# Gate weights split earlier, and the second half of the first four units taken unit by unit

## The reference

```
x = x + 0.5 * rmsnorm(swiglu(rmsnorm(x, g[4]), w_in, w_out), g[5])      # feed-forward
gate = sigmoid(rmsnorm(x, g[6]) @ ple_w_gate)                           # 1024 x 1024
x = x + rmsnorm(gate * (p @ ple_w_proj), g[7])                          # 256 x 1024
```

```
h = h + 0.5 * swiglu(rms_norm(h, norm_ffn2), w_ffn2_in, w_ffn2_out)
gate = sigmoid(rms_norm(h, norm_ple) @ w_ple_gate)
h = h + gate * (p @ w_ple_proj)
```

## Time and profile before

| | |
|---|---|
| median of 3 executions | 1807.92 us (1805.59 to 1808.70) |
| the profiled execution | 1809.24 us, of which the span of the trace is 1807.4 us |
| TensorE busy | 1726.5 us, 96% of the span, 11967 products |
| VectorE busy | 1091.2 us, 60% |
| ScalarE busy | 882.4 us, 49% |
| GpSimd busy | 174.9 us, 10% |
| splits | 528 of each kind: 1053 ns on ScalarE, 1264 ns on VectorE |

### The profile page before, as it was taken

How to read it: one execution, slowest core, us unless ns; L and a number is a source line. 1 busy time by engine, 2 the same in 40 slices (tenths; PEclk the granted TensorE clock), 3 DMA queues, 4 the chain that set the end, 5 groups by cost and what they waited for, 6 DMA issues and landing times.

```text
span 1807.4 us, 28143 instructions
## 1 busy us (share of the span) xinstructions
PE 1726.5 (96%) x11967; PEld 1577.3 (87%) x11967; DVE 1091.2 (60%) x1410; ACT 882.4 (49%) x1370; POOL 174.9 (10%) x192
## 2 busy tenths in 40 slices
PE   7999999999998999999999999999999997999996
PEld 6899799899986998979789997799989887899995
DVE  4455667678766544658565555655566575755555
ACT  4344456544565455452554445544454434444444
POOL 0000001219002002910010000100000000000000
PEclk9999999999999999999999999999999998999999
DMA  6655443455554444531445554455545331454552
GB/s 228 233 191 187 167 160 131 167 187 186 187 175 155 183 167 148 186 117 47 175 144 200 186 185 165 160 208 189 197 158 187 117 117 62 166 208 174 187 197 74
DMA packets 51084, 300.97 MB, mean 167 GB/s; under 512 B 6072, under 2 KB 12688, under 8 KB 17168
## 3 DMA queue, kind: packets, MB, share of 16 engines
q1 hardware_dynamic: 50800, 298.66, 46.4%
q0 software_dynamic: 160, 0.52, 0.1%
HBM read 298.08 MB, written 1.09 MB: 166 GB/s over the span
## 4 chain that ended last, share of the span: by engine, by line
PE 81%; ACT 7%; DVE 7%; issue 2%; DMA 2%; POOL 1%; SPq 0%; DVEq 0%; POOLq 0%; ACTq 0%
PE PS L1816 77%; DVE wlo L1122 2%; PE PS L1819 2%; ACT whi L647 2%; ACT wk L690 1%; DVE xn L1211 1%; POOL st L539 1%; ACT SC L779 1%; DMA SC<-in_pT 1%; DMA raw<-in_w 1%; PE PS L1941 1%; DVE X L1203 0%; POOL st L532 0%; ACT xn L702 0%; PE PS L2121 0%
## 5 line engine op out<-in xcount | busy, mean ns | idle before, releaser
L1122 DVE TENSOR_TENSOR wlo<-raw,whi 128x1024 fp32r<-128x1024 f32 x528 | 662.4, 1264 | 442.6 <-ACT whi L647 441.7
L647 ACT ACTIVATE whi<-raw 128x1024 fp32r<-128x1024 f32 x528 | 549.7, 1053 | 411.9 <-PE PS L1816 253.3
L1816 PE MATMUL PS<-xhi,whi 128*128 128x256 f32 x2536 | 723.3, 286 | 7.0 <-DVE wlo L1122 6.2
L1816 PE MATMUL PS<-xhi,wlo 128*128 128x256 f32 x2536 | 717.4, 284 | 0.0
L1816 PE MATMUL PS<-xlo,whi 128*128 128x256 f32 x2536 | 710.9, 284 | 0.0
L1816 PEld LDWEIGHTS PS<-xhi,whi 128*128 128x128 f32 x2536 | 488.4, 193 | 15.5 <-DVE wlo L1122 9.0
L1816 PEld LDWEIGHTS PS<-xhi,wlo 128*128 128x128 f32 x2536 | 488.2, 193 | 0.0
L1816 PEld LDWEIGHTS PS<-xlo,whi 128*128 128x128 f32 x2536 | 484.7, 193 | 2.0
L1816 PE MATMUL PS<-whi,hhi 128*128 128x512 f32 x544 | 170.1, 394 | 2.4 <-DVE wlo L1122 2.4
L1816 PE MATMUL PS<-wlo,hhi 128*128 128x512 f32 x544 | 168.7, 391 | 0.0
L1816 PE MATMUL PS<-whi,hlo 128*128 128x512 f32 x544 | 168.6, 391 | 0.0
(11 more groups left out here) (261 smaller groups left out, 1444.4 us busy)
## 6 DMA issues: line engine op xcount, KB each, us to landing
raw<-in_w SPq DMA_DIRECT2D x264, 1024.0 KB, 4.8
gr<-in_rows SPq DMA_DIRECT2D x23, 512.0 KB, 3.7
SC<-scratch SPq DMA_DIRECT2D x1, 2048.0 KB, 11.9
SC<-scratch SPq DMA_DIRECT2D x2, 1024.0 KB, 11.6
X<-in_x SPq DMA_DIRECT2D x2, 512.0 KB, 4.8
xn<-in_sc SPq DMA_DIRECT2D x2, 512.0 KB, 6.9
out<-xn SPq DMA_DIRECT2D x2, 512.0 KB, 2.7
SC<-in_pT SPq DMA_DIRECT2D x3, 256.0 KB, 4.4
```

The lines of the kernel that those rows point to most:

```text
L647: a.activation(whi[:, u % NSPLIT, :], raw[:, u // 2 % NRAW, u % 2 * HU:u % 2 * HU + HU], ACT.Copy).then_inc(s_hi, 1)
L1122: v.tensor_tensor(wlo[:, u % NSPLIT, :], src, hi.bitcast(f32), SUB).then_inc(s_lo, 1)
L1816: return pe.matmul(o, l, r, start=start, stop=stop)
```

## The change

It has three parts.

1. In the gated layers, the splits of the first two gate units move. ScalarE issues them behind position 1 of the table, that is behind the squares of half 0, and VectorE behind position 2, that is behind the sum of half 0. The hook at position 5 keeps only the copies of the projection (on ScalarE). `ahead.done` is set by hand behind the step, to what the removed call had left.
2. In `run` and in the attention's `values`, half 1 of the first four units no longer has two passes: it waits for the high and the low part of the rows and then takes each unit with all three products. Half 0 is unchanged.
3. In `meanwhile`, steps 3, 7 and 11 return early, so the four unread products ahead of the transposes of half 0 are gone, in each of the three gated layers.

```diff
--- before.py
+++ after.py
@@ -749,8 +749,9 @@
             def ple(layer):
                 k = (3, 7, 11)[layer]
 
-                def project():
-                    linear(f"proj{layer}", 2, head=2, tail=0)
+                v0 = LAST[f"proj{layer}"] - 1
+
+                def projected():
                     for h in range(2):
                         if h:
                             q.wait_ge(s_used, LAST[f"proj{layer}"] + 1)
@@ -762,7 +763,8 @@
                     y_ready(q, k + 1, h)
                     a.activation(xn[:, h, :], flat(4 + 2 * h), ACT.Sigmoid).then_inc(s_gate, 1)
 
-                settle(k, {5: project})
+                settle(k, {1: lambda: use(v0), 5: projected})
+                ahead.done = v0 + 1
                 linear(f"gate{layer}", 8, head=4, tail=2, finish=lambda: evict_hi(k, 1))
                 gate(0)
                 settle(k + 1, {0: lambda: gate(1)})
@@ -1267,7 +1269,9 @@
                 def rest():
                     evict_lo(k, 1)
 
-                take_turns(k, steps, {5: lambda: linear(f"proj{layer}", 2, head=2, tail=0)})
+                v0 = LAST[f"proj{layer}"] - 1
+                take_turns(k, steps, {2: lambda: use(v0)})
+                ahead.done = v0 + 1
                 linear(f"gate{layer}", 8, head=4, tail=2, finish=rest)
                 take_turns(k + 1, steps)
 
@@ -1830,7 +1834,9 @@
                         between()
                     if by_half is not None:
                         q.wait_ge(s_xhi, n_ev(by_half, h, 0))
-                    for low in (False, True) if by_half is not None else (None,):
+                        if h:
+                            q.wait_ge(s_xlo, n_ev(by_half, h, 0))
+                    for low in (False, True) if by_half is not None and not h else (None,):
                         if low:
                             q.wait_ge(s_xlo, n_ev(by_half, h, 0))
                         for n, (u, ahi, alo, first, end) in enumerate(parts):
@@ -1910,7 +1916,9 @@
                     return
                 if k in (4, 8, 12):
                     turn_idle(b, s_gate, 2 * GATED.index(k) + h + 1)
-                if k in POST and k not in (3, 7):
+                if k in (3, 7, 11):
+                    return
+                if k in POST:
                     if k in GATED:
                         turn_idle(b, s_yg, n_yg(k, h))
                     turn_idle(b, s_sq, n_sq(k, h, 0))
@@ -2041,9 +2049,11 @@
                     w_n = cols.stop - cols.start
                     per = HU // w_n
                     for h in range(2):
-                        for low, n in [(b, n) for b in (False, True) for n in ns] if by_half is not None else [(None, n) for n in ns]:
-                            if low is not None:
-                                q.wait_ge(s_xlo if low else s_xhi, n_ev(by_half, h, n // 2))
+                        for low, n in [(b, n) for b in (False, True) for n in ns] if by_half is not None and not h else [(None, n) for n in ns]:
+                            if low is not True and by_half is not None:
+                                q.wait_ge(s_xhi, n_ev(by_half, h, n // 2))
+                            if low is not False and by_half is not None:
+                                q.wait_ge(s_xlo, n_ev(by_half, h, n // 2))
                             if low is False and h == 0 and n == 2:
                                 transposed(1, 1)
                             u = LAST[name] - 8 // per + 1 + n
```

## The result

| | before | after |
|---|---|---|
| median of 5 executions | 1807.92 us (1803.86 to 1809.38) | 1797.74 us (1794.95 to 1800.88) |
| ratio, 95% interval | | 0.9939 [0.9923, 0.9956] |
| the same pair in a later set (11 and 6 executions) | 1808.79 us | 1794.64 us, ratio 0.9925 [0.9913, 0.9937] |
| span of the trace | 1807.4 us | 1793.2 us (later set: 1794.5) |

The change is faster by 11.0 us in the first set (1807.92 x 0.0061; 8.0 to 13.9) and by 13.6 us in the second (11.4 to 15.7). The forecast was 8.4 us. The sign and the mechanisms came as told; the size did not: 8.4 lies near the lower end of the first interval and outside the second. By the ratio the first set gives 1807.92 x 0.9939 = 1796.9 us, just under the range; the median of its five executions, 1797.74, lies just inside.

What follows compares the result with a forecast made beforehand. TensorE, with 81% of the chain, was taken as the bound. Gains of 3.6 (gates' second half), 1.1 (attention's values), 3.4 (splits) and 0.3 (layer 2) sum to 8.4 us: 1807.92 to 1799.5 us, range 1797 to 1803.8.

Steps and rivals of the forecast that it cites:

- The bound and the places: TensorE bounds the kernel; its waits lie between projection and gate, and behind the first four units of gates and attention's values.
- Second half unit by unit: Gates and attention's values: buffers come free sooner, closing gaps before the fifth unit; 3.6 us in gates, 1.1 in values.
- that sign of error: Layer 0's fifth-unit transfer lands after its buffer is free, delaying the split some 0.4 us of 1.35 us to spare.
- The splits: Between projection and gate, layers 0 and 1: moved splits let the gate start 1.7 us earlier each, 3.4 us in all.
- the cover: Before the gate: half 1's sum, even with GpSimd slowed, is done by 1113.0, about when ScalarE squares it at 1112.9.
- Layer 2: Third gated layer: without the unread products ahead of the transposes, the eviction starts sooner; gain 0.3 us.
- The clock, "I take 0": Gates: removing the unread products lets no lower TensorE clock reach the second half; cost taken as 0.
- The gain's upper bound, 9 us: Whole kernel: the bounds of the terms were said to give gains from about 7 to 9 us.
- A: Gates of layers 0 and 1: late squares or sum make the splits gain nothing; gain 5.0 us, 1802.9; chance 0.14.
- B: Second half of the gates: transfers hold the fifth unit, gap stays in layers 0 and 1; 1801.9; chance 0.10.
- C: Whole kernel: attention absorbs its gain, splits gain nothing, one gap stays; gain 2.7 us, 1805.2; chance 0.10.
- D: All three gates: without unread products TensorE's clock falls into products that set the end; slower, 1810.4; chance 0.04.

Runs made afterwards that it cites:

- part 3 alone: Kernel before, with only the unread products ahead of the first half's transposes removed in the gated layers: 1807.46 us against 1808.45, ratio 1.0006.
- products put back: Changed kernel with the unread products ahead of the first half's transposes restored: 1797.25 us, ratio 0.9942.
- the kernel with the moved sigmoids: Kernel before, next feed-forward's first splits moved behind the first sigmoid on ScalarE and both halves' multiplications on VectorE, layers 0 and 1: 1812.9 us, ratio 1.0028.
- the one with the splits alone: Kernel before, with only the splits of the first two gate units moved and the unread products kept: 1804.2 us, ratio 0.9984.
- after, again: The changed kernel itself, unaltered, run and profiled a second time in a later set: 1794.64 us, ratio 0.9925.

## Why the prediction was right and where it was wrong

- **The bound and the places** were right: beside what the clock moves, nothing was gained outside the attention's values and the gated layers (the feed-forward parts behind layers 0 and 1 take 215.0 and 191.5 us in both kernels).
- **Second half unit by unit:** the gaps closed for the reason given. The buffer was free 1.62 us into the half (told: 1.6). In layer 0 the fifth unit's split waited for its transfer and came 1.9 us into the half, some 0.3 us late (told: 0.4 of 1.35 to spare), so that sign of error occurred without harm. The term was mis-sized, a smaller error than the one below: 3 x 1.20 + 1.1 = 4.7 us by the idle times of the rows, 3 x 1.47 + 1.4 = 5.8 by the distances.
- **The splits:** told 1.7 us in each of two layers. Measured at the first gate product 1.85 in layer 1, and in layer 0 1.76 by the first profiles (11.52 and 9.76) and 2.40 by the second (12.04 and 9.64). The path was the one described: copies, then eviction. GpSimd's roots beside VectorE took 1.16 and 1.18 us, longer than the 0.84 expected, and the cover held: the squares of half 1 started 7.9 us behind the projection, not 8.3. With the lock that the Trainium skill (SBUF — State Buffer, Who interferes with whom) states I had worked out 1.6 us. The trace agrees with the rule: the two lengthened root operations end 0.17 and 0.08 us behind the VectorE instructions beside them (1098.21 + 1.16 behind 1096.85 + 2.35, 1100.62 + 1.18 behind 1100.32 + 1.40). The gain was 1.85 all the same.
- **Layer 2:** told 0.3, measured 0.43 to 0.45 us (part 3 alone, and products put back).
- **The clock, "I take 0":** right for the change, as far as three profiles can tell: the first of after spoke against it, the second and the kernel with part 3 alone for it.
- **The step that failed** is the end of the path: the sum stopped at the last gate product and put what lies behind it at nothing, without a reason. What stood between it and GpSimd's root, a sigmoid held by a transfer for a split of the next part, was not read, though the rows were in the trace of before. There the change brought 1.3 to 2.5 us in layer 1 (6.59 and 6.02 less 4.08 and 4.74) and 0.5 in layer 0, together 1.8 to 3.0 us. I had written that a term could fall short by a cover that fails, never that bringing things forward also frees what is late behind. The gain's upper bound, 9 us, had room in the splits alone (2 x 2.1 us) and in no other term; the lower, 7 us, did not follow from the bounds either, since splits that gain nothing leave 5.0.
- With the terms as measured (layer 0 by the first profiles) the sum is 5.8 + 3.6 + 0.4 + 1.8 to 3.0 = 11.6 to 12.8 us, beside the marks' 12.7 (11.0 by the means).
- **Rivals:** A, B and C did not come. D's mechanism showed in one of two profiles, cost 1.33 us in layer 1 and 1.36 in layer 2 there, and came in the kernel with the moved sigmoids (layer 1) and in the one with the splits alone (layer 0) too, which both keep the unread products. So their removal is not needed for it; that the removal never makes a fall more likely is not shown by so few profiles.

**Still open:** why the transfer for the next feed-forward part takes 5.63 to 6.89 us in some executions and 4.75 in another; by the table of transfers this alone, with an unchanged moment of issue, puts the sigmoid of layer 1 at 37.01, 36.43 or 35.79 us, and it holds it at 31.82 in one profile of after where 30.92 was free. Nor was it tried what decides in which execution a fall of the clock comes.

## What to carry to other kernels

Value a wait of TensorE by the distance from the start at which the next product was due to the start at which it came, not by the idle time of its row. Follow an advance past the end of the products to the next place where all meet: the work behind may be held by something that comes forward with it, and its gain, or its price, belongs to the sum. Where one profile shows a low clock at a new place, profile the same kernel again before naming a cause.

## What the runs showed of the hardware

TensorE's granted clock falls to its lower level (1.2 of 2.4 GHz) for a few us at some places of this program (about 80, 216, 540, 800, 904, 1112, 1144, 1412 and, longer, 1508 us in the kernel before), at those of 80, 800 and 1112 us in one execution of the same kernel and not in another. Where such a fall lies on products that set the end it cost 1.15 us (stretch C), 1.33 to 1.39 us (B with after, again; layers 1 and 2 with after) and up to 2.6 us (A); where TensorE would have waited anyway it cost nothing (the one at 1112 us: the third unit at 15.02 us instead of 15.01). So two profiles of one kernel differ by some 3 us in code that nobody touched, and parts of a change worth 1 to 2 us can be read from distances between marks but not from totals.

The first of the two GpSimd operations of a reciprocal root, on 128 numbers, took 0.29 us alone and 1.16 to 1.18 us beside VectorE's splits and normed rows. The transfer of 1 MB for the next feed-forward part, asked at the same point of the program, took 5.63, 6.27 and 6.86 us in three executions.
